# Decode keys laid out by kv head through a copy in DRAM and turned on VectorE

## The reference

```python
    s_c = jnp.einsum('bqkgd,bckd->bkgqc', q, kc, preferred_element_type=f32) * scale \
        - slopes[:, :, None, None] * (tq[:, None] - c_mid[None, :])
    p_c = masked_softmax(s_c, c_end[None, :] <= q_pos[:, None], -1)
    o_c = jnp.einsum('bkgqc,bckd->bqkgd', p_c, vc)
...
    score = jnp.where(valid, imp + jnp.where(forced, FORCE_BONUS, 0.0), -1.0)
    _, idx = lax.top_k(score, min(SLC_TOPK, ns))
...
    gk = gather(ks, idx)
    gv = gather(vs, idx)
    pos = idx[..., None] * SLC_BLOCK + jnp.arange(SLC_BLOCK)
    dist = (tq[:, None, None] - pos.astype(f32))[:, :, None]
    s_s = jnp.einsum('bqkgd,bkqnsd->bkgqns', q, gk, preferred_element_type=f32) * scale \
        - slopes[:, :, None, None, None] * dist
    mask_s = (pos <= q_pos[:, None, None])[:, :, None]
    p_s = masked_softmax(s_s, mask_s, (-2, -1))
    o_s = jnp.einsum('bkgqns,bkqnsd->bqkgd', p_s, gv)
...
    s_w = jnp.einsum('bqkgd,bwkd->bkgqw', q, kw, preferred_element_type=f32) * scale \
        - slopes[:, :, None, None] * (tq[:, None] - w_pos.astype(f32)[None, :])
    mask_w = (wp <= tp) & (tp - wp < WINDOW) & (wp >= 0)
    p_w = masked_softmax(s_w, mask_w, -1)
    o_w = jnp.einsum('bkgqw,bwkd->bqkgd', p_w, vw)
...
    o = gates[:, :, 0, :, :, None] * o_c + gates[:, :, 1, :, :, None] * o_s + gates[:, :, 2, :, :, None] * o_w
...
def nsa_sample(h, past, win_buf, w_in, w_cmp_k, w_cmp_v, w_o):
    B, Q, _ = h.shape
    q, kv, gates = nsa_project(h, w_in)
    P = past.shape[1]
    full = jnp.concatenate([past, kv[:, :, :4]], axis=1)
    kc = compress(full[:, :, 0], w_cmp_k)
    vc = compress(full[:, :, 1], w_cmp_v)
    ks = to_slc_blocks(full[:, :, 2])
    vs = to_slc_blocks(full[:, :, 3])
    wb = win_buf.shape[1]
    win = jnp.concatenate([win_buf, kv[:, :, 4:6]], axis=1)
    w_pos = P - wb + jnp.arange(wb + Q)
    q_pos = P + jnp.arange(Q)
    o = nsa_attend(q, gates, q_pos, kc, vc, ks, vs, win[:, :, 0], win[:, :, 1], w_pos)
    keep = min(WINDOW, wb + Q)
    return o.reshape(B, Q, Q_W) @ w_o, kv[:, :, :4], win[:, wb + Q - keep:]
```

## Time and profile before

| | us |
|---|---|
| median of 3 runs | 1444.57 (1444.19 to 1446.05) |
| profiled execution, own time | 1449.33 |
| span of the profiled execution | 1447.4 |
| PE busy | 1406.6 (97%) |
| DVE busy | 341.8 (24%) |
| ACT busy | 162.7 (11%) |
| POOL busy | 38.3 (3%) |
| DMA packets, bytes | 95121, 475.59 MB |

### The profile page before, as it was taken

One profiled execution on the slowest core, in us unless ns is written; L12 is line 12 of the kernel. 1 busy time (PEld: TensorE's weight loads), 2 busy tenths in 40 slices (PEclk: granted clock), 3 DMA queues, 4 the chain that ended last, 5 costly groups with the idle time before them and its releaser, 6 DMA issues.

```text
span 1447.4 us, 31668 instructions
## 1 busy us (share of the span) xinstructions
PE 1406.6 (97%) x14007; PEld 830.7 (57%) x14007; DVE 341.8 (24%) x790; ACT 162.7 (11%) x416; POOL 38.3 (3%) x57
## 2 busy tenths in 40 slices
PE   9999999999999999999998999999998999999997
PEld 7887787888876568435434336336444336336434
DVE  5122222324237872202020011002020111002021
ACT  3000000001024652000000000000000000000101
POOL 3000000001000001000000000000000000000000
PEclk9999999999999999999999999999999999999999
DMA  9967774446353793899999999999999999999994
GB/s 326 358 276 270 262 261 156 156 184 204 117 191 112 225 259 160 344 371 421 414 410 425 424 408 425 425 385 418 423 405 424 425 409 424 425 364 413 424 426 197
DMA packets 95121, 475.59 MB, mean 329 GB/s; under 512 B 9944, under 2 KB 35720, under 8 KB 70143
## 3 DMA queue, kind: packets, MB, share of 16 engines
q1 hardware_dynamic: 92855, 467.57, 82.0%
q0 software_dynamic: 2128, 5.99, 1.3%
HBM read 469.65 MB, written 12.71 MB: 333 GB/s over the span
## 4 chain that ended last, share of the span: by engine, by line
PE 91%; DMA 4%; DVE 3%; issue 1%; SPq 0%; ACT 0%; DVEq 0%; ACTq 0%
PE banks L1237 34%; PE banks L1296 15%; PE banks L790 14%; PE banks L808 7%; PE banks L857 5%; DMA ring<-in_w_moe_gate 4%; PE banks L1164 2%; PE banks L1338 2%; PE banks L941 1%; PE banks L771 1%; PE banks L1000 1%; PE banks L1015 1%; DVE arena L2141 1%; PE banks L1031 1%; PE banks L1091 1%; PE banks L958 1%
## 5 line engine op out<-in xcount | busy, mean ns | idle before, releaser
L1237 PE MATMUL banks<-ring,arena 128*32 128x512 f32 (+1 forms) x5376 | 521.6, 541 | 6.1 <-DMA ring<-in_w_moe_gate 6.1
L1237 PEld LDWEIGHTS banks<-ring,arena 128*32 128x32 f32 x5376 | 179.3, 110 | 320.4 <-issue 312.6
L1296 PE MATMUL banks<-ring,arena 128*32 128x256 f32 x4704 | 262.8, 383 | 17.1 <-DVE arena L2141 11.8
L1296 PEld LDWEIGHTS banks<-ring,arena 128*32 128x32 f32 x4704 | 166.3, 111 | 111.2 <-issue 17.8
L790 PE MATMUL banks<-hT,ring 128*128 128x264 f32 x896 | 202.6, 387 | 0.0
L790 PEld LDWEIGHTS banks<-hT,ring 128*128 128x128 f32 x896 | 169.3, 190 | 36.9 <-issue 8.4
L2122 DVE TENSOR_TENSOR xT<-banks,xT 128x264 f32<-128x264 f32 x56 | 24.2, 433 | 453.4 <-PE banks L1338 453.4
L808 PE MATMUL banks<-arena,ring 128*128 128x264 f32 x448 | 101.5, 387 | 0.0
L808 PEld LDWEIGHTS banks<-arena,ring 128*128 128x128 f32 x448 | 84.6, 190 | 19.2 <-issue 5.0
L857 PE MATMUL banks<-hT,ring 128*128 128x264 f32 x256 | 57.5, 386 | 0.0
L2136 DVE TENSOR_TENSOR arena<-arena,banks 128x512 f32<-128x512 f32 (+1 forms) x42 | 24.0, 597 | 138.6 <-PE banks L1237 138.6
(11 more groups left out here) (336 smaller groups left out, 809.8 us busy)
## 6 DMA issues: line engine op xcount, KB each, us to landing
ring<-in_w_moe_gate SPq DMA_DIRECT2D x64, 1792.0 KB, 17.2
ring<-in_w_moe_up SPq DMA_DIRECT2D x64, 1792.0 KB, 16.7
ring<-in_w_moe_down SPq DMA_DIRECT2D x32, 2048.0 KB, 19.4
ring<-in_w_moe_down SPq DMA_DIRECT2D x32, 1536.0 KB, 20.4
arena<-in_cache_kv SPq DMA_DIRECT2D x64, 256.0 KB, 8.0
ring<-in_cache_kv SPq DMA_DIRECT2D x128, 128.0 KB, 2.2
ring<-in_w_ffn_gate SPq DMA_DIRECT2D x7, 2048.0 KB, 7.9
ring<-in_w_ffn_up SPq DMA_DIRECT2D x7, 2048.0 KB, 13.4
```

The costliest lines, as they stand in the source:

```text
L1237: last = mm(banks[CT * q:CT * (q + 1), 2 * t + part, 0:PART_W[part]], xe[:, c, CT * t:CT * (t + 1)], cols.rearrange("p (j s e) -> p s j e" ...
L1296: last = mm(banks[CT * q:CT * (q + 1), 6 + place // 2, 256 * (place % 2):256 * (place % 2 + 1)], mh[:, t, at:at + CT], w[:, r, 256 * h:256 ...
```

## The change

A part's keys are laid out anew in DRAM first. During layer 0, POOL issues 72 DMAs from DRAM to DRAM (64 of one page, 8 of a window), which write `key_rows`: for each part and kv head, rows of 64 numbers (256 B). `key_part` then loads each kv head of a part into its own 32 partitions (4 DMAs, each 32 by 64 runs of 256 B). DVE's `turn_keys` transposes the 32x32 blocks in place, 1024 columns at a time, 4 for a part, 24 in all: 20 stand between the projections, 4 after them. A partition then holds one of 32 numbers of one kv head, so a product of 128 partitions covers four kv heads and half of the 64 numbers; a second query layout `qd` serves it. PE's 192 transposes and the 48 copies to `KT` go, the 12 score rounds stay.

Other steps move: the 36 transposes of the new keys and values (`natural_rows`) and the 8 of the compressed rows go in between the projections, and their copies from DVE to ACT; part of the query layout goes to ACT; SP reads the page numbers of four value chunks ahead, and its wait for free slots is now on `sc_done`; SP waits for all copies before part 0; score rounds 8 to 11 stand behind the scores of the first prompt pair.

```diff
-        qz = qz_f.rearrange("p (a b m) -> p a b m", a=2, b=TS)
+        qz, qd = (qz_f[:, 512 * n:512 * (n + 1)].rearrange("p (a b m) -> p a b m", a=2, b=TS) for n in range(2))
...
-        kpart = [ring[:, KEY_SLOT[p], :].rearrange("p (i c n) -> p i c n", i=4, c=4) for p in range(6)]
+        kpart = [ring[:, KEY_SLOT[p], :].rearrange("p (i x h t) -> p i x h t", i=4, x=16, h=2) for p in range(6)]
...
+        key_rows = nc.dram_tensor("key_rows", (6, NKV, 4, WIN, HD), F32).ap()
...
+        EARLY_IDS = 4
...
             def key_part(p):
-                piece, j = divmod(p, 2)
-                for i in range(4):
-                    b = 2 * i + j
-                    if piece < 2:
-                        load_pages(b, piece, kpart[p][:, i], 2 * KVW, 3 * KVW, kv_in[2 * p])
-                    else:
-                        sp.dma_start(kpart[p][:, i], state_win[0, b, :, 0].rearrange("(c p) k d -> p c (k d)", p=P)
-                                     ).then_inc(kv_in[2 * p], 16)
+                for a in range(NKV):
+                    sp.dma_start(ring[32 * a:32 * (a + 1), KEY_SLOT[p], :].rearrange("p (x d) -> p x d", d=HD),
+                                 key_rows[p, a].rearrange("i (x t) d -> t (i x) d", t=32)).then_inc(kv_in[2 * p], 16)
...
-                        at = b * NPAGE + c
-                        pid = sp.value_load(pages[0:1, at:at + 1], min_val=0, max_val=cache_kv.shape[1] - 1)
+                        pid = early[c][b] if c < EARLY_IDS else page_id(b, c)
...
+            sp.wait_ge(key_copied, 16 * 9 * TS)
             sp.wait_ge(gu_ps, FS * NG)
             key_part(0)
...
+            early = [[page_id(b, c) for b in range(TS)] for c in range(EARLY_IDS)]
             for k in range(12):
                 if k % 2 == 0:
-                    sp.wait_ge(kt_ps, 8 * (k // 2 + 1))
+                    sp.wait_ge(sc_done, 2 * (k // 2 + 1))
...
+            gp.wait_ge(small_in, 3 * 16)
+            for p in range(6):
+                piece, j = divmod(p, 2)
+                for i in range(4):
+                    b = 2 * i + j
+                    if piece == 2:
+                        gp.dma_start(key_rows[p, :, i].rearrange("a t d -> t a d"), state_win[0, b, :, 0]
+                                     ).then_inc(key_copied, 16)
+                        continue
+                    for n in range(4):
+                        at = b * NPAGE + 4 * piece + n
+                        pid = gp.value_load(pages[0:1, at:at + 1], min_val=0, max_val=cache_kv.shape[1] - 1)
+                        gp.dma_start(key_rows[p, :, i, P * n:P * (n + 1)].rearrange("a t d -> t a d"),
+                                     cache_kv[0, bass.ds(pid, 1), :, 2].rearrange("o t k d -> (o t) k d")
+                                     ).then_inc(key_copied, 16)
             add_squares(1, NC - 1)
-            gp.wait_ge(nat_act, 5)
-            gp.wait_ge(nat_dve, 4)
...
+                if n == 3:
+                    pe.wait_ge(picked_all, 2 * TS)
+                    for b in range(TS):
+                        last = tr(banks[:, 4 + b // 4, P * (b % 4):P * (b % 4 + 1)],
+                                  cmp_rows[:, 2 * b:2 * b + 2].rearrange("p m d -> p (m d)"), ident)
+                        if b % 4 == 3:
+                            last.then_inc(xc_ps, 1)
+                if n >= 17:
+                    for u in range(2):
+                        natural_rows(2 * (n - 17) + u)
...
-            def key_round(r):
-
-                p, a = divmod(r, 2)
-                if a == 0:
-                    pe.wait_ge(kv_in[2 * p], part_value(p))
-                for i in range(4):
-                    if r:
-                        pe.wait_ge(kt_dve if i % 2 else kt_act, 2 * (r - 1) + i // 2 + 1)
-                    for c in range(4):
-                        last = tr(banks[:, 4 + i, P * c:P * (c + 1)], kpart[p][:, i, c, P * a:P * (a + 1)], ident)
-                    last.then_inc(kt_ps, 1)
-
             def score_round(r):
 
-                p, a = divmod(r, 2)
+                p, h = divmod(r, 2)
                 piece, j = divmod(p, 2)
-                pe.wait_ge(kt_act, 2 * (r + 1))
-                pe.wait_ge(kt_dve, 2 * (r + 1))
-                if r == 0:
-                    pe.wait_ge(kc_act, 8)
-                if r == 4:
-                    pe.wait_ge(cs_in, 1)
+                pe.wait_ge(kt_dve, 4 * (p + 1))
                 if r == 8:
                     pe.wait_ge(vcz_ready, 2)
                 for i in range(4):
                     rows = slice(32 * i, 32 * (i + 1))
-                    last = mm(banks[rows, piece, :], qz[:, a, 2 * i + j, rows], KT[:, r % 2, i], start=(j == 0 and a == 0),
-                              stop=(j == 1 and a == 1), skip_group_check=True)
+                    last = mm(banks[rows, piece, :], qd[:, h, 2 * i + j], kpart[p][:, i, :, h], start=(j == 0 and h == 0),
+                              stop=(j == 1 and h == 1), skip_group_check=True)
                 last.then_inc(sc_done, 1)
...
-            for r in range(ROUNDS):
-                key_round(r)
-                if r == 0:
-                    compressed_scores()
-                    prompt_compressed()
-                else:
-                    if r == 1:
-                        prompt_compressed_rows()
-                    score_round(r - 1)
-                if r == 3:
-                    pe.wait_ge(gates_ready, 1)
-                    pe.wait_ge(dec_max, 1)
-                    mm(banks[:, 3, 64:112], K("spread_b", TS), gn[0:TS, 2, :], start=True, stop=True).then_inc(gd_ps, 1)
-                if r == 5:
-                    pe.wait_ge(imp_in, 1)
-                    mm(banks[:, 3, 0:NSLC_D], K("same_kv"), sm16[:, 0:NSLC_D], start=True, stop=True).then_inc(imp_ps, 1)
-            score_round(ROUNDS - 1)
-
-
-            pe.wait_ge(cs_w, 1)
-            for i in range(2):
-                last = tr(banks[:, 7, P * i:P * (i + 1)], pcp_f[:, P * i:P * (i + 1)], ident)
-            last.then_inc(pdt_ps, 1)
+            compressed_scores()
+            pe.wait_ge(vcp_sb, 1)
+            mm(banks[:, 2, 0:KVW], K("blk_of", NCMP_P), vcn_p[0:NCMP_P, :], start=True, stop=True).then_inc(rep_ps, 1)
+            prompt_compressed()
+            for r in range(4):
+                score_round(r)
...
             prompt_scores(0)
+            pe.wait_ge(imp_in, 1)
+            mm(banks[:, 3, 0:NSLC_D], K("same_kv"), sm16[:, 0:NSLC_D], start=True, stop=True).then_inc(imp_ps, 1)
+            for r in range(8, ROUNDS):
+                score_round(r)
+            pe.wait_ge(cs_in, 1)
             compressed_value_rows()
+            prompt_scores(1)
+            selected_weight_columns()
             compressed_weight_columns()
-            selected_weight_columns()
-            prompt_scores(1)
+            pe.wait_ge(cs_w, 1)
+            for i in range(2):
+                last = tr(banks[:, 7, P * i:P * (i + 1)], pcp_f[:, P * i:P * (i + 1)], ident)
+            last.then_inc(pdt_ps, 1)
...
+            def turn_keys(p, i):
+
+                if i == 0:
+                    dve.wait_ge(kv_in[2 * p], part_value(p))
+                blocks = kpart[p][:, i].rearrange("p x h t -> p (x h) t")
+                V.transpose(blocks, blocks).then_inc(kt_dve, 1)
+
+            TURNS = {1: 1, 2: 1, 3: 1, 4: 1, 5: 1, 6: 1, 8: 1, 9: 1, 10: 1, 11: 1, 12: 1, 14: 1, 15: 1, 16: 2, 17: 2, 18: 2, 19: 1}
+            turned = 0
             order_queries(0)
             inverse_root(1)
...
+                for _ in range(TURNS.get(n, 0)):
+                    turn_keys(*divmod(turned, 4))
+                    turned += 1
...
-            compressed_columns()
+            decode_compressed()
+            gates()
             repeat_values()
-            for r in range(ROUNDS):
-                for i in (1, 3):
-                    dve.wait_ge(kt_ps, 4 * r + i + 1)
-                    if r >= 2:
-                        dve.wait_ge(sc_done, r - 1)
-                    V.tensor_copy(KT[:, r % 2, i], banks[:, 4 + i, :]).then_inc(kt_dve, 1)
-                if r == 1:
-                    compressed_softmax()
-                if r == 2:
-                    decode_compressed()
-                if r == 3:
-                    compressed_weights()
-                if r == 4:
-                    decode_importance()
-                if r == 5:
-                    selected_scores(0)
-                if r == 6:
-                    decode_choice()
-                if r == 7:
-                    drop_block(0)
-                    selected_max(0)
-                if r == 8:
-                    selected_scores(1)
-                    drop_block(1)
-                if r == 9:
-                    selected_max(1)
-                    tt(sm[:, 1:2], sm[:, 13:14], sm[:, 14:15], ALU.min).then_inc(dec_max, 1)
-                if r == 10:
-                    selected_sum()
+            for i in range(4):
+                turn_keys(5, i)
+            selected_scores(0)
```

(11 more changed lines are left out.)

210 lines of the change are left out of this document (103 added, 107 removed).

## The result

| | before | after |
|---|---|---|
| median of the runs beside each other | 1444.19 us (1443.42 to 1446.05, 9 runs) | 1448.78 us (1446.96 to 1452.9, 9 runs) |
| ratio after/before | | 1.0035 (95%: 1.0027 to 1.0044) |
| span of the profiled execution | 1447.4 | 1444.9 |

The change costs 4.6 us by the two medians. I had said 1432 with 1421 to 1449; 1448.78 lies just inside that range, on the wrong side of the time before. The two profiled executions point the other way (1447.4 before, 1444.9 after), so spans alone mislead here.

The account below looks back on a forecast made before the run. PE's key transposes (23.8 us) bound the 38.8 us before the window scores; with them gone, DVE's four terms put `window_max` at 453.2 instead of 466.15, SP's limit agreeing. 13 us off gave 1432 us, range 1421 to 1449.

Parts of the forecast that it names:

- The step that failed: Dense stage, beside POOL's copies: weights are fetched far ahead into seven slots, so no wait of PE was counted.
- sums over 280 us: From 51 to 331 us: the copies need 77 us of DMA time (60 to 154), where 106 us are idle.
- GpSimd's issues: POOL's 72 copies during layer 0: 2.2 ns a run, 175 us in all, from about 51 to 226 us.
- The rival of a slow GpSimd: POOL's copies at 5 ns a run end at 364 us, PE stops at projection 1; 1450 us; chance 0.14.
- First: Steps on DVE ahead of part 5, after the projections: DVE comes to the turns of part 5 at about 431.4 us.
- Second: Part 5's load: issued at 421 us, 12.8 us at 25 ns a packet, there at 435, a wait of 3.6 us.
- Third: DVE's four turns of part 5: 1.7 us each, 6.8 us together (2.4 to 8.8), done at 441.8 us.
- a sign of being wrong: Between the projections: DVE waiting for a key part there would show the prediction wrong; no size given.
- Fourth: Rest of the decode softmax on DVE after the turns: 11.4 us, so `window_max` starts at 453.2, 13 us earlier.
- Fifth: SP's value chunks after part 5: SP free at 429.5 us, so the values can follow a shift of 13.3 us.
- The sum: Whole kernel: 13 us off the profiled 1449.33 gives 1436.3; the median goes from 1444.57 to 1431.6, said as 1432.
- the key parts arriving late: Key part loads before the decode scores: at 33 ns a packet 1441 us, at 40 ns 1463; chance 0.18.

Follow-up runs that it names:

- the paced run: Against the changed kernel, GpSimd starts its key copies only when the 8 MB window copy has landed; 1436.04 us.
- the reorder: Against the changed kernel, DVE does first-half scores, importance and the prompt's compressed softmax ahead of the four turns of part 5; 1448.25 us.

## Why the prediction was wrong, step by step

**The step that failed** is "The seven weight slots are fetched far ahead, so I count no wait of PE here." It is true of the weights, for which PE waits nowhere in the dense stage, and I asked it of the weights alone. The runs showed a wait of 12.1 us for the compress pages in its place. SyncE's queue also carries the compress pages, which have three places and are wanted every 15.4 us, and the 8 MB window copy. I had compared sums over 280 us (77 us of DMA time against 106 idle). As a sum it was more than safe: from 40 to 320 us GpSimd's queue took 13.2% of the engines' time, against 0.4% before, so the copies cost some 36 us and not 77, and the paced run has them hidden with no wait. But in every trace here the page loads that come next behind the window copy are held until 45 to 56 us after its issue, and the key copies met it where only about 2 us were left (estimate above). The chain is: page loads slowed, window copy 7.4 us later and 5.3 us slower, page loads behind it free at 131 and not 118 us, PE 12.5 us late and 2.6 more by the clock. Without the copies the time falls by 14.7 us, with them alone it rises by 14.0, and two different ways to keep them apart from the window copy give back 12.7 (paced) and 14.3 (window copy moved). That the meeting of the two copies is the cause is shown from both sides. How it holds two queues at once is not. None of my rivals had it: they priced the copies at GpSimd and the runs at the DMA engines, not what waits behind the window copy.

**GpSimd's issues** were overestimated. A page copy took 0.74 us for 512 runs, against 0.54 for 32: 0.4 ns a run, where I took 2.2. The last copy was issued at 199.4 us, for all the 40.2 us of hold, where I had said 226. The rival of a slow GpSimd was never near.

**First** held. DVE is through with the steps ahead of part 5 at 445.56, which is 430.5 without the 15.1 us of the dense stage; I said 431.4.

**Second** was too short by 4.2 us. The first of the four loads is issued at 435.6 (420.5 without the 15.1; I said 421). The part is there at 454.25, which is 439.15, and I said 435. A run of 256 B took what I had taken: in the middle of the key loads some 155 GB/s move, which through 16 engines is 26 ns each. But around part 5 other packets are on the way. DMA queues of the changed kernel from 436 to 454 us (packets, MB, share):

```profile
q1 hardware_dynamic: 8256, 2.10, 89.5%
q0 software_dynamic: 512, 1.62, 24.1%
```

The 512 are GpSimd's six stores of the keys and values in natural order, issued from 441.28 to 444.01 us: 0.241 x 18 = 4.3 us of all the engines. That fits the size, but no run took the stores away, so it is argued and not shown. What is shown is the weight of the length of the runs: in runs of 4096 B the wait is 1.96 us, and the time falls by 7.5.

**Third**: a turn of 1024 columns took 1.235 us, four of them 4.62 us and not 6.8. I leaned on strided transposes of before. My estimate from the Trainium skill ("Vector Engine (DVE) Microarchitecture Reference", section 3.8), 4.3 us for four, was the closer one. The trace comes near it, not quite to it: 1.235 us is 1.2 ns a column, where the estimate has 1.04. The turns hidden under the projections cost PE nothing: it is busy for 61.00 of 61.00 us, though DVE did wait 4.79 and 3.14 us for parts 0 and 1. I had taken such a wait for a sign of being wrong; the two fitted into the time in which DVE had nothing to do.

**Fourth**: from the end of the turns to the window scores 11.2 us, said 11.4.

**Fifth**: SyncE is free at 443.3 (428.2 without the 15.1; I said 429.5). Page numbers and four chunks take 461.94 + 17.7 - 443.3 = 36.3 us in sum (I said 35.7), and the last chunk is issued by 517.66, which is 502.6; I said 504. That both chains end together is shown by the reorder, where the window scores came 3.7 us earlier and PE then waited for value chunks instead.

**The sum.** The stretch gained 11.2 of the 13 us. What I had not counted is what follows. In the changed kernel PE stands idle for 8.63 us at part 5 and the clock falls behind it (0.58 from 460 to 465, 0.50 from 475 to 480 us). In the kernel before the granted clock stays at 1.00 there in the second profile and fell in the first. Set against the second, the prompt's attention loses 2.7 us (72.1 for 69.3); that this is the clock is argued from the rows. So the expert stage starts 15.1 - 11.2 + 2.7 = 6.6 us later by these terms, and 589.6 - 583.2 = 6.4 by the traces. The expert matmuls then span 808.0 us and not 810.7, a gain that I had not counted and whose cause is open. That leaves 4 us at the end of the two spans (1444.9 for 1440.9), and the medians say 4.6. I had left the stage behind the decode scores as it was in an execution whose clock fell there, and took the 4.8 us off to come to the median. So the clock's fall was in my time before and no longer in my time after, and I promised 13 us where 8 to 10 were there (9.7 without the copies, 8.9 with the window copy moved, 7.8 with the copies paced).

Of the rivals, the key parts arriving late was the nearest: part 5 did come late, but by 4.2 us, and with runs at 26 ns and not at 33 or 40. Its cure, longer runs, is worth 7.5 us. That 1448.78 still lies in my range is luck: a wait that I had not foreseen filled the place of the rivals that I had.

## What to carry to other kernels

Before background transfers are counted as hidden because the DMA engines have idle time in sum, write down for each queue what is issued behind what, how long the largest transfer holds the next items, and who wants them when. Here one 8 MB copy made no wait at the end of a batch, 12.9 us in the middle of one, and 12.1 us at the end of a batch with key copies beside it. Where a layout is free to choose, choose it by the length of the runs that the later load reads, and let the operation that reads the result undo the order: it cost nothing here and gave 7.5 us. And profile the kernel before twice before a difference of a few microseconds is carried from a trace to a median.

## What the runs showed of the hardware

- While the 8 MB copy from DRAM to DRAM in eight rows passes, the DMA share is 0.48 to 0.56 in the stretches with no other large transfer. Each row cut in two, it was 0.51 to 0.56.
- The next loads of SyncE's queue were held until 50.0 us after its issue (before), 55.3 us (changed kernel) and 45.5 us (no key copies beside it, more loads behind it). GpSimd's issue of key copies stood still for 40.2 us beside it, and for 2.9 us at the same place without it.
- Loads into 32 partitions: runs of 256 B move at 155 GB/s (26 ns each). In runs of 4096 B it was 210 GB/s from 360 to 380 us, and 224 from 438 to 448 us with other traffic included. Sixteen times longer runs gave less than half again, not sixteen times.
- The key copies cost GpSimd 0.74 us for 512 runs of 256 B. Its queue has 6352 packets and 18.57 MB, against 2128 and 5.99 before: 4224 packets for 12.58 MB, 3.0 KB each, so a packet carries some 12 runs.
- Reading PSUM with a stride of 32 elements took the same 0.71 us as reading it straight.
- TensorE's granted clock was 0.50 (1.2 GHz) for 10 us around the end of a wait of 12.1 us. In two executions of the kernel before, the same stretch took 75.0 us at a mean of 0.91 and 69.3 at 1.00.
- A transpose of 32x32 blocks over 1024 adjacent columns takes 1.235 us, 1.2 ns a column, where strided ones of before took 1.7 to 2.1.
